# Attention: mask and row maximum in one VectorE instruction per head, and half of the probabilities' copy on ScalarE

## The reference

```
scores = einsum(q, k of this block and the block before) * 64 ** -0.5      # 16 heads, 4 key heads, head size 64
valid  = (q_pos - k_pos >= 0) & (q_pos - k_pos < 128) & (k_pos >= 0)
scores = where(valid, scores, -1e30)
probs  = softmax(concat([scores, sink of the head]))[..., :-1]
out    = einsum(probs, v of the same two blocks)
```

## Time and profile before

| | us |
|---|---|
| median of three timed runs (lowest, highest) | 2120.76 (2119.61, 2121.04) |
| the profiled execution's own time | 2119.99 |
| its span | 2118.1 |
| TensorE busy | 2006.9 (95%) |
| VectorE busy | 1354.6 (64%) |
| ScalarE busy | 748.2 (35%) |
| GpSimd busy | 198.3 (9%) |

### The profile page before, as it was taken

The page is one execution under the profiler, slowest core; times in us unless marked ns, Lnnn a source line. Parts: engine busy times, 40 slices in busy tenths (PEclk is TensorE's granted clock), DMA queues, the critical chain, the costliest instruction groups (busy, mean ns, idle before and its releaser), DMA issues.

```text
span 2118.1 us, 27334 instructions
## 1 busy us (share of the span) xinstructions
PE 2006.9 (95%) x9446; PEld 1646.9 (78%) x9446; DVE 1354.6 (64%) x1935; ACT 748.2 (35%) x1369; POOL 198.3 (9%) x232
## 2 busy tenths in 40 slices
PE   6779999999999988999999997999999999999799
PEld 6758888888888867888866685788888888888587
DVE  4886666666666676466579548766666666665942
ACT  3452222333222243243268534333222223332421
POOL 1300000000000043010035311000000000000600
PEclk8889999999999999999999998999999999999999
DMA  4233222233222241121010012333222232334211
GB/s 174 82 99 100 83 83 86 85 99 94 85 84 88 81 178 36 65 105 50 0 41 1 11 60 85 90 100 94 79 89 84 83 90 74 99 99 173 69 42 50
DMA packets 214750, 173.17 MB, mean 82 GB/s; under 512 B 8608, under 2 KB 196384, under 8 KB 214688
## 3 DMA queue, kind: packets, MB, share of 16 engines
q1 hardware_dynamic: 212960, 166.08, 24.7%
q10 hardware_dynamic: 1728, 6.29, 0.8%
HBM read 159.75 MB, written 12.58 MB: 81 GB/s over the span
## 4 chain that ended last, share of the span: by engine, by line
PE 84%; DVE 9%; POOL 3%; issue 2%; ACT 1%; SPq 1%; DMA 0%; ACTq 0%; DVEq 0%; POOLq 0%
PE ps L285 13%; PE ps L287 13%; PE ps L286 13%; PE ps L684 13%; PE ps L686 13%; PE ps L685 13%; PE ps L1364 1%; PE ps L347 1%; PE ps L1306 1%; DVE w_ple_gate_lo L280 1%; POOL probs L1356 1%; DVE t_lo L929 1%; DVE H L1048 1%; DVE small L1315 1%; PE ps L1384 1%
## 5 line engine op out<-in xcount | busy, mean ns | idle before, releaser
L1004 DVE TENSOR_TENSOR H<-H,ps 128x512 f32<-128x512 f32 x320 | 218.1, 685 | 141.8 <-PE ps L287 141.8
L285 PE MATMUL ps<-wd_hi,ffn_a_hi 128*128 128x512 f32 x704 | 275.9, 392 | 9.1 <-DVE H L1004 8.5
L286 PE MATMUL ps<-wd_lo,ffn_a_hi 128*128 128x512 f32 x704 | 274.9, 391 | 0.0
L287 PE MATMUL ps<-wd_hi,ffn_a_lo 128*128 128x512 f32 x704 | 274.9, 390 | 0.0
L684 PE MATMUL ps<-t_hi,s_hi 128*128 128x512 f32 x528 | 207.4, 393 | 20.4 <-DVE t_lo L929 19.0
L685 PE MATMUL ps<-t_lo,s_hi 128*128 128x512 f32 x528 | 206.6, 391 | 0.0
L686 PE MATMUL ps<-t_hi,s_lo 128*128 128x512 f32 x528 | 206.4, 391 | 0.0
L770 ACT ACTIVATE s_hi<-s_raw 128x512 fp32r<-128x512 f32 x176 | 111.3, 633 | 232.7 <-DVE s_raw L893 229.2
L893 DVE TENSOR_TENSOR s_raw<-s_raw,a_raw 128x512 f32<-128x512 f32 x88 | 60.9, 692 | 191.2 <-DMA s_raw<-in_w_ff_gate 145.8
L794 ACT ACTIVATE m<-ps 128x512 f32<-128x512 f32 x44 | 25.9, 589 | 405.0 <-PE ps L686 405.0
L285 PEld LDWEIGHTS ps<-wd_hi,ffn_a_hi 128*128 128x128 f32 x704 | 132.5, 188 | 40.3 <-DVE H L1004 9.2
(11 more groups left out here) (199 smaller groups left out, 4246.3 us busy)
## 6 DMA issues: line engine op xcount, KB each, us to landing
a_raw<-in_w_ff_gate SPq DMA_DIRECT2D x88, 256.0 KB, 2.9
a_raw<-in_w_ff_up SPq DMA_DIRECT2D x88, 256.0 KB, 3.1
s_raw<-in_w_ff_up SPq DMA_DIRECT2D x88, 256.0 KB, 2.9
s_raw<-in_w_ff_gate SPq DMA_DIRECT2D x88, 256.0 KB, 3.2
wd_raw<-in_w_ff_down SPq DMA_DIRECT2D x44, 512.0 KB, 4.1
residual_spill<-H SPq DMA_DIRECT2D x16, 512.0 KB, 2.6
raw<-in_w_ple_gate SPq DMA_DIRECT2D x16, 512.0 KB, 5.4
back<-residual_spill SPq DMA_DIRECT2D x16, 512.0 KB, 5.9
```

What stands on the lines that cost most here:

```text
L285: pe.matmul(out_, lhs[0], rhs[0], start=first, stop=False)
L286: pe.matmul(out_, lhs[0], rhs[1], start=False, stop=False)
L287: return pe.matmul(out_, lhs[1], rhs[0], start=False, stop=last)
L1004: dve.tensor_tensor(dst, dst, ps[:, 4 + n % 4, :], ALU.add).then_inc(F["summed"][n % 4], 1)
```

## The change

The scores' matmuls now start their PSUM sums themselves (`start=True`), and neither TensorE nor ScalarE puts a mask there. In `softmax_max` VectorE takes one instruction per head of 256 columns, which writes (scores + mask) * -1/8 back into PSUM and gives the minimum of that and of the negated sink; the exp takes scale -1. The copy of the turned probabilities is split by bank: VectorE copies the even half, ScalarE the odd half, in its queue right behind exp(n + 1). The identity in the reduced format goes, and the mask stays in float32.

```
 def scores(pe, n):
...
-            m2 = mask_r[:, min(t, 1), :].unsqueeze(1).to_broadcast([P, 2, 2 * P])
-            for c in range(2 if n < 2 else 1):
-                pe.matmul(banks(2 * par)[:, c * HALF:(c + 1) * HALF].rearrange("p (h k) -> p h k", h=2),
-                          ident_r[:, :], m2, start=True, stop=False, skip_group_check=True)
-            if n >= 2:
-                pe.wait_ge(at_masked, n - 1)
...
-                                 qo[half, t, k * P:(k + 1) * P], kT[half, t:t + 2, g, :], start=False, stop=m >= 2,
-                                 skip_group_check=True)
+                                 qo[half, t, k * P:(k + 1) * P], kT[half, t:t + 2, g, :], start=True, stop=True)
 def softmax_max(dve, n):
...
-            dve.tensor_reduce(neg_row_max[par], banks(2 * par).rearrange("p (h k) -> p h k", h=GQA), AX.X, ALU.max,
-                              negate=True).then_inc(at_max, 1)
-            dve.wait_ge(at_max, n + 1)
-            gs = slice(GQA * g, GQA * (g + 1))
-            dve.scalar_tensor_tensor(out=neg_max[par], in0=neg_row_max[par], scalar=HEAD ** -0.5, in1=neg_sinks[:, gs],
-                                     op0=ALU.mult, op1=ALU.min).then_inc(at_neg_max, 1)
+            for m in range(GQA):
+                head = banks(2 * par)[:, m * 256:(m + 1) * 256]
+                last = dve.tensor_tensor_reduce(head, head, mask[:, min(t, 1), :], -HEAD ** -0.5,
+                                                neg_sinks[:, GQA * g + m:GQA * g + m + 1], ALU.add, ALU.min,
+                                                neg_max[par][:, m:m + 1])
+            last.then_inc(at_neg_max, 1)
             dve.wait_ge(at_neg_max, n + 1)
             dve.tensor_tensor(sink_gap[par], sinks_placed[:, gs], neg_max[par], ALU.add).then_inc(at_gap, 1)
 def softmax_exp(act, n):
...
-                last = act.activation(probs[g][:, sl], banks(2 * par)[:, sl], ACT.Exp, scale=HEAD ** -0.5,
+                last = act.activation(probs[g][:, sl], banks(2 * par)[:, sl], ACT.Exp, scale=-1.0,
...
-        def mask_odd_heads(act, n):
...
 def turn_probs(pe, n):
             pe.wait_ge(at_normed, n + 1)
-            if n >= 1:
-                pe.wait_ge(at_pt, n)
             for k in range(8):
+                if n >= 1 and k % 4 == 0:
+                    pe.wait_ge((at_pt_even, at_pt_odd)[k // 4], n)
...
+        def probs_copy_even(dve, n):
             dve.wait_ge(at_turned, n + 1)
             if n >= 2:
                 dve.wait_ge(at_pv, n - 1)
-            dve.tensor_copy(pt[n % 2][:, :, :].rearrange("p a b -> p (a b)"), banks(4)).then_inc(at_pt, 1)
+            dve.tensor_copy(pt[n % 2][:, 0:4, :].rearrange("p a b -> p (a b)"), ps[:, 4, :]).then_inc(at_pt_even, 1)
+
+        def probs_copy_odd(act, n):
+            act.wait_ge(at_turned, n + 1)
+            if n >= 2:
+                act.wait_ge(at_pv, n - 1)
+            act.activation(pt[n % 2][:, 4:8, :].rearrange("p a b -> p (a b)"), ps[:, 5, :], ACT.Copy).then_inc(at_pt_odd, 1)
...
 ScalarE's queue:
             softmax_exp(act, 0)
-            act.wait_ge(at_probs, 1)
-            mask_odd_heads(act, 2)
             q_act(act, PAIRS - 1, 1)
             for n in range(1, STEPS_A):
                 softmax_exp(act, n)
-                if n + 2 < STEPS_A:
-                    act.wait_ge(at_probs, n + 1)
-                    mask_odd_heads(act, n + 2)
+                probs_copy_odd(act, n - 1)
                 if n >= 4 and n % 2 == 0:
                     att_out(act, n // 2 - 2)
                 if n % 3 == 1 and n // 3 < KD:
                     cut_hi(act, BASE["o"], n // 3, w_o[0][:, n // 3, :])
+            probs_copy_odd(act, STEPS_A - 1)
```

More of the change, by code:

```diff
@@ L74, in constants @@
         "rope_cos": np.cos(angle), "rope_sin": np.sin(angle),
-        "mask_unit": np.concatenate([mask[:, 0], mask[:, 1], np.eye(P), np.zeros((P, D - 5 * P))], axis=1),
+        "mask_unit": np.concatenate([mask[:, 0], mask[:, 1], np.zeros((P, D - 4 * P))], axis=1),
     }
@@ L198, in trunk @@
                    at(100, ("kT", [P, TILES + 1, KV_HEADS, P], F32), ("V", [P, TILES + 1, GROUP], F32),
-                      ("mask_r", [P, 2, 2 * P], F32R), ("ident_r", [P, P], F32R),
+                      ("mask", [P, 2, 2 * P], F32),
                       ("cos", [P, TILES, 32], F32), ("sin", [P, TILES, 32], F32)),
@@ L1282, in trunk @@
         pt = [tmp[:, :].rearrange("p (k c) -> p k c", k=KD), E["pt1"]]
-        mask_r, ident_r = B["mask_r"], B["ident_r"]
+        mask = B["mask"]
         neg_sinks_set = sem("neg_sinks_set")
-        at_scores, at_max, at_neg_max, at_gap = [sem(f"att_{x}") for x in ("scores", "max", "neg_max", "sink_gap")]
+        at_scores, at_neg_max, at_gap = [sem(f"att_{x}") for x in ("scores", "neg_max", "sink_gap")]
         at_probs, at_sum, at_recip, at_normed = [sem(f"att_{x}") for x in ("probs", "sum", "recip", "normed")]
-        at_turned, at_pt, at_pv, at_out = [sem(f"att_{x}") for x in ("p_turned", "pt", "pv", "out")]
-        at_masked = sem("att_mask_placed")
+        at_turned, at_pv, at_out = [sem(f"att_{x}") for x in ("p_turned", "pv", "out")]
+        at_pt_even, at_pt_odd = [sem(f"att_pt_{x}") for x in ("even", "odd")]
         def scores(pe, n):
@@ L1306, in scores @@
                 last = pe.matmul(ps[:, 2 * par + m % 2, (m // 2) * 256:(m // 2 + 1) * 256].rearrange("p (b c) -> p b c", b=2),
-                                 qo[half, t, k * P:(k + 1) * P], kT[half, t:t + 2, g, :], start=False, stop=m >= 2,
-                                 skip_group_check=True)
+                                 qo[half, t, k * P:(k + 1) * P], kT[half, t:t + 2, g, :], start=True, stop=True)
             last.then_inc(at_scores, 1)
         def softmax_max(dve, n):
-            g, par = n % 4, n % 2
+            t, g, par = n // 4, n % 4, n % 2
+            gs = slice(GQA * g, GQA * (g + 1))
             dve.wait_ge(at_scores, n + 1)
-            dve.tensor_reduce(neg_row_max[par], banks(2 * par).rearrange("p (h k) -> p h k", h=GQA), AX.X, ALU.max,
-                              negate=True).then_inc(at_max, 1)
-            dve.wait_ge(at_max, n + 1)
-            gs = slice(GQA * g, GQA * (g + 1))
-            dve.scalar_tensor_tensor(out=neg_max[par], in0=neg_row_max[par], scalar=HEAD ** -0.5, in1=neg_sinks[:, gs],
-                                     op0=ALU.mult, op1=ALU.min).then_inc(at_neg_max, 1)
+            for m in range(GQA):
[4 more added lines that the diff above has]
+            last.then_inc(at_neg_max, 1)
             dve.wait_ge(at_neg_max, n + 1)
@@ L1333, in softmax_exp @@
                 sl = slice(m * 256, (m + 1) * 256)
-                last = act.activation(probs[g][:, sl], banks(2 * par)[:, sl], ACT.Exp, scale=HEAD ** -0.5,
+                last = act.activation(probs[g][:, sl], banks(2 * par)[:, sl], ACT.Exp, scale=-1.0,
                                       bias=neg_max[par][:, m:m + 1], accum_out=sums[:, GQA * g + m:GQA * g + m + 1])
             last.then_inc(at_probs, 1)
-        def mask_odd_heads(act, n):
-            m2 = mask_r[:, min(n // 4, 1), :].bitcast(F32).unsqueeze(1).to_broadcast([P, 2, 2 * P])
-            act.activation(ps[:, 2 * (n % 2) + 1, :].rearrange("p (h k) -> p h k", h=2), m2, ACT.Copy).then_inc(at_masked, 1)
         def softmax_recip(dve, n):
@@ L1360, in turn_probs @@
             pe.wait_ge(at_normed, n + 1)
-            if n >= 1:
-                pe.wait_ge(at_pt, n)
             for k in range(8):
+                if n >= 1 and k % 4 == 0:
+                    pe.wait_ge((at_pt_even, at_pt_odd)[k // 4], n)
                 last = pe.transpose(banks(4)[:, k * P:(k + 1) * P], probs[n % 4][:, k * P:(k + 1) * P], ident[:, :])
             last.then_inc(at_turned, 1)
-        def probs_copy(dve, n):
+        def probs_copy_even(dve, n):
             dve.wait_ge(at_turned, n + 1)
@@ L1370, in probs_copy @@
                 dve.wait_ge(at_pv, n - 1)
-            dve.tensor_copy(pt[n % 2][:, :, :].rearrange("p a b -> p (a b)"), banks(4)).then_inc(at_pt, 1)
+            dve.tensor_copy(pt[n % 2][:, 0:4, :].rearrange("p a b -> p (a b)"), ps[:, 4, :]).then_inc(at_pt_even, 1)
[4 more added lines that the diff above has]
+            act.activation(pt[n % 2][:, 4:8, :].rearrange("p a b -> p (a b)"), ps[:, 5, :], ACT.Copy).then_inc(at_pt_odd, 1)
         def values(pe, n):
             t, g = n // 4, n % 4
-            pe.wait_ge(at_pt, n + 1)
+            pe.wait_ge(at_pt_even, n + 1)
+            pe.wait_ge(at_pt_odd, n + 1)
             if n == 0:
@@ L1688, in q_cut @@
                 if isinstance(i, int) and i == 0 and p == 0:
-                    cut_hi(act, BASE["mask"], 0, mask_r[:, :, :].rearrange("p m k -> p (m k)"), columns=slice(0, 4 * P))
+                    cut_hi(act, BASE["mask"], 0, mask[:, 0, :], columns=slice(0, 2 * P))
                 if isinstance(i, int):
@@ L1819, in q_cut @@
                     dve.wait_ge(hi_done, BASE["mask"] + 1)
```

(6 more changed lines are left out.)

## The result

| | before | changed |
|---|---|---|
| median of 12 runs (lowest, highest), us | 2119.78 (2118.58, 2122.84) | 2124.18 (2121.97, 2127.15) |
| the profiled execution's span, us | 2118.1 | 2122.9 |
| turn(3) to turn(24), 21 steps, us | 75.90 | 80.64 |
| turn(24) to turn(29), us | 16.68 | 16.22 |
| turn(29) to turn(31), us | 5.54 | 6.56 |

The ratio is 1.0019, 95% interval 1.0010 to 1.0028. That is slower, as forecast, by 4.4 us between the medians (4.0 by the ratio), where 6.2 us were forecast; it is just about the 4.2 us that the prediction took as the least that can be told from none, but the interval excludes none. The median of before is now of twelve runs and 1.0 us lower than that of the first three.

The account below looks back on a forecast made before the run. Bound: a latency chain containing VectorE's w_o cut, and TensorE without it; the change closes a longer loop through ScalarE. Terms +5.55, -0.2, +1.1, -0.6, +0.3 give +6.2 us, so 2127.0 us, range 2121.5 to 2133.

Parts of the forecast that it names:

- turn(3) to turn(24): 21 attention steps between TensorE's transposes of steps 3 and 24, with w_o cuts: 81.45 us for 75.90, +5.55.
- turn(24) to turn(29): Five attention steps without w_o cuts, between transposes of steps 24 and 29: 16.50 us for 16.68, -0.2.
- turn(29) to turn(31): Last two steps' transposes, now held by the loop through ScalarE's copy: 6.60 us for 5.54, +1.1.
- a head on VectorE; the maximum in all: One of four new 256-column VectorE instructions, 0.43 us; all four up to the next VectorE instruction, 1.97 for 1.53.
- the loop with both cuts: Three-step loop through ScalarE's half copy and both engines' w_o cuts: 11.35 us, 11.85 with the output copy.
- the last copy: VectorE's copy at the attention's very end, 512 columns instead of 1024: -0.6 us.
- the head: Start of the attention, where the first maximum gives its sink gap 0.44 us later: +0.3, between -0.3 and +1.
- Rival 2: VectorE's accumulator output is free, 0.34 us a head, maximum 1.60: total +3.3, 2124 us; chance 0.17.
- Rival 1: Nothing overlaps on VectorE, 0.58 us a head, maximum 2.56: total +12.3, 2133 us; chance 0.14.
- the half rate: VectorE's four new instructions run at half rate, maximum 3.04 us: +17 in all, 2138 us; chance 0.03.
- rival 3: ScalarE runs so far behind that its copies delay nothing: -4.7, 2116 us; -2.1 with maximum 1.97; chance 0.13.
- the old loop without a cut: Chain maximum, norm, turn without VectorE's w_o cut; 7.16 us for two steps under Rival 1.

Follow-up runs that it names:

- e2: Kernel before with only the copy split between VectorE and ScalarE, mask and maximum as before: 2126.86 us, ratio 1.0039.
- e1: Kernel before with only VectorE's new mask-and-maximum instructions, copy whole on VectorE, none on ScalarE: 2120.31 against 2119.18 us, ratio 1.0004.
- e3: Changed kernel with ScalarE's half copy moved last in its step, behind output copy and w_o cut: 2118.53 us, ratio 0.9997.
- e4: Changed kernel with only ScalarE's w_o cut moved ahead of the half copy, output copy still behind it: 2118.36 us, ratio 0.9998.
- e5: e3 with VectorE's w_o cut in thirds, one a step right behind the reciprocals: 2113.26 against 2119.34 us, ratio 0.9969.
- e7: Changed kernel, ScalarE's order kept, with VectorE's w_o cut in thirds behind the reciprocals: 2118.22 us, ratio 0.9997.
- e8: e5 with VectorE's thirds of the w_o cut moved behind its half copy: 2139.78 against 2118.12 us, ratio 1.0095.

## Why the prediction was right

By its own steps:

| step | forecast, us | measured, us |
|---|---|---|
| a head on VectorE; the maximum in all | 0.43; 1.97 | 0.405; 1.88 |
| the loop with both cuts, without and with the output copy | 11.35; 11.85 | 11.2 to 11.3; 11.7 |
| turn(3) to turn(24) | +5.55 | +4.74 |
| turn(24) to turn(29) | -0.2 | -0.46 |
| turn(29) to turn(31) | +1.1 | +1.02 |
| the last copy (turn(31) to the low part of the first tile: 5.08, now 4.59) | -0.6 | -0.49 |
| the head (sinks to turn(3): 18.36, now 18.59) | +0.3 | +0.23 |
| sum | +6.2 | +5.0 |

The spans differ by 4.8, since the attention starts 0.27 us earlier in the second execution. The mechanism is shown, not only fitted. The half copy alone costs no less than the whole change (e2), VectorE's part alone is 1.1 us over before, which cannot be told from nothing (e1), and moving the copy behind two other instructions of its queue removes the loss (e3). The stretches summed before e1 to e4 came within 0.3 us of those measured (76.6, 82.85, 75.0 and 75.3 expected; in e1 partly by luck, as said), those before e5 to e7 within 1.0.

What was mis-sized is the price of a head. I added 0.09 to the 0.34 of a plain instruction, and it costs 0.405; over the whole maximum that makes 0.09 us, seven times in the stretch, 0.6 of the 0.8 us by which it was missed. Rival 2, the free accumulator, named 2124, which is nearest to the time measured, but its step (0.34 a head) is wrong. Its time fits in part because the median of before moved by 1.0; as a difference, the sum of +5.0 lies between its +3.3 and my +6.2, as 0.405 lies between 0.34 and 0.43. Rival 1 and the half rate fall with the 0.405, and rival 3 with ScalarE's 17.3 us of waiting. Rival 3 has a slip: with a maximum of 1.97 the old loop without a cut is 7.70 - 1.13 = 6.57 for two steps, so the five steps there take 3.28 and not TensorE's 3.10, and the case is about -1.2, not -2.1. The same term was left out again before e3. The strict form of the Trainium skill's rule on the drain ("VectorE: DVE Perf Modes", section "The DRAIN you can't avoid"), weighed in the prediction, does not hold here either, if the end of a row is taken for the end of the instruction: the next start lies 0.08 before the end of the row in front.

What the prediction did not see is the cheaper cure. It named the cut between maximum and reciprocals as part of the bound of before, and did not ask whether it had to stand there.

## What to carry to other kernels

An instruction moved to another engine brings its wait with it. What counts is what stands behind it in that queue, and whether a loop closes, not the busy time, which fell on three of the four engines here and rose on none. In an in-order queue, work that is ready goes ahead of work that waits. Sum the loops over as many steps as they span: that sum, from rows of before, gave 81.45 us for this kernel's stretch of 80.64.

## What the runs showed of the hardware

VectorE and GpSimd can hold each other up at SBUF. A VectorE instruction with two inputs in SBUF that starts 0.17 us before GpSimd's multiplication lengthens it from 1.89 to 2.07 us (e5); one that starts 0.43 after it waits almost to its end and takes 1.83 for 0.48 (e8). The new instruction, with one input in PSUM, runs beside norm at its usual 0.49, and norm beside it at 1.89 in the changed kernel. The Trainium skill, "SBUF — State Buffer", section "Who interferes with whom", states this: a VectorE instruction with both inputs in SBUF contends with a GpSimd instruction that reads SBUF, the order of issue decides who waits, and one with at most one SBUF input, outside the modes that use two ports, does not contend. The traces agree in who waits; in e5, though, norm waits 0.18 us of the 0.32 for which the two rows overlap. In e5 the 0.18 us lie in a loop of two steps, so they are some 1.9 us of its stretch, which came out 1.0 over its expectation; that this is the whole reason was not tried.

A head's instruction with its accumulator read takes 0.06 to 0.07 us more of VectorE's queue than a plain one of 256 columns (0.405 against 0.34 in the earlier trace rows), though the read's row is 0.14 long. How much of that is the read and how much the other instruction, whose own row is 0.49 for 0.42, no run separates.
